# A two-layer mLSTM and GLA decoder step in one core: x stored in pieces, weight tiles requested one unit sooner, the samples' states requested over more units, GLA's last exponentials behind the gate's eviction

## The reference, cut to what matters

```python
for i in range(DEPTH):                       # DEPTH = 2, D_MODEL = 1024, D_FF = 2816
    h = rms_norm(x, g_pre_mix[i])
    mix, state = mlstm_mixer(h, ...) if i % 2 == 0 else gla_mixer(h, ...)
    x = x + rms_norm(mix, g_post_mix[i])
    h = rms_norm(x, g_pre_ffn[i])
    x = x + rms_norm(swiglu(h, w_gate[i], w_up[i], w_down[i]), g_post_ffn[i])

def swiglu(x, w_gate, w_up, w_down):
    return (silu(x @ w_gate) * (x @ w_up)) @ w_down
```

## Time and profile before

| | |
|---|---|
| median of 3 runs | 2727.17 us (2725.6 to 2729.15) |
| the profiled execution | 2726.81 us, of which 2725.0 us are the span from its first to its last instruction |
| PE busy | 2635.9 us, 97% of the span |
| ACT, DVE busy | 1009.2 us (37%), 1495.0 us (55%) |
| granted TensorE clock | mean 0.985 of full speed |
| DMA | 331.25 MB, mean 122 GB/s |

### The profile page before, as it was taken

How to read it: one execution, slowest core, us unless ns; L and a number is a source line. 1 busy time by engine, 2 the same in 40 slices (tenths; PEclk the granted TensorE clock), 3 DMA queues, 4 the chain that set the end, 5 groups by cost and what they waited for, 6 DMA issues and landing times.

```text
span 2725.0 us, 38277 instructions
## 1 busy us (share of the span) xinstructions
PE 2635.9 (97%) x15999; PEld 2383.3 (87%) x15999; DVE 1495.0 (55%) x2301; ACT 1009.2 (37%) x1439; POOL 0.2 (0%) x4
## 2 busy tenths in 40 slices
PE   7999999999999999999999999999999999999996
PEld 6899898877978998899899987998886979999996
DVE  5644475555466763356654775327676377444435
ACT  4443355432343333344423343335452334222222
POOL 0000000000000000000000000000000000000000
PEclk9999999999999999999999999999999999999998
DMA  5454454444434233443232333443335333322222
GB/s 192 137 178 143 137 170 138 132 131 143 139 112 132 85 108 103 154 131 97 90 100 93 114 117 111 139 150 115 106 103 182 112 114 127 113 84 79 86 79 84
DMA packets 181831, 331.25 MB, mean 122 GB/s; under 512 B 19580, under 2 KB 99068, under 8 KB 181660
## 3 DMA queue, kind: packets, MB, share of 16 engines
q1 hardware_dynamic: 181660, 328.81, 37.3%
HBM read 272.48 MB, written 56.28 MB: 121 GB/s over the span
## 4 chain that ended last, share of the span: by engine, by line
PE 84%; DVE 7%; ACT 4%; DMA 2%; issue 2%; SPq 0%; ACTq 0%; DVEq 0%
PE ps L837 75%; PE ps L996 2%; DMA w_stage<-w_down_in 2%; ACT w_hi L1104 1%; DVE w_lo L1411 1%; DVE Y L1504 1%; DVE n_xs L1507 1%; DVE Y L1471 1%; DVE evicted L1455 1%; PE ps L1077 1%; PE ps L949 1%; ACT hid_hi L1168 1%; PE ps L937 1%; PE ps L931 1%; PE ps L1026 1%
## 5 line engine op out<-in xcount | busy, mean ns | idle before, releaser
L837 PE MATMUL ps<-HH,w_lo 128*128 128x288 f32 (+1 forms) x3696 | 1025.2, 332 | 17.0 <-DVE HL L1905 7.4
L837 PE MATMUL ps<-HH,w_hi 128*128 128x288 f32 (+1 forms) x3696 | 1010.5, 328 | 0.0
L837 PE MATMUL ps<-HL,w_hi 128*128 128x288 f32 (+1 forms) x3696 | 1010.4, 328 | 0.0
L837 PEld LDWEIGHTS ps<-HH,w_lo 128*128 128x128 f32 x3696 | 631.7, 189 | 79.2 <-DVE w_lo L1411 17.6
L1411 DVE TENSOR_TENSOR w_lo<-w_stage,w_hi 128x1024 fp32r<-128x1024 f32 x396 | 483.6, 1221 | 367.4 <-ACT w_hi L1104 366.2
L837 PEld LDWEIGHTS ps<-HL,w_hi 128*128 128x128 f32 x3696 | 630.3, 189 | 49.3
L837 PEld LDWEIGHTS ps<-HH,w_hi 128*128 128x128 f32 x3696 | 630.4, 189 | 47.4 <-issue 0.2
L1104 ACT ACTIVATE w_hi<-w_stage 128x1024 fp32r<-128x1024 f32 x396 | 416.3, 1052 | 428.8 <-PE ps L837 292.8
L837 PE MATMUL ps<-hid_hi,w_lo 128*128 128x288 f32 (+1 forms) x1056 | 298.4, 337 | 39.4 <-issue 18.4
L1471 DVE TENSOR_TENSOR Y<-ps,Y 128x512 f32<-128x512 f32 (+1 forms) x320 | 226.9, 720 | 152.6 <-PE ps L837 152.2
L837 PE MATMUL ps<-hid_hi,w_hi 128*128 128x288 f32 (+1 forms) x1056 | 293.3, 333 | 0.0
(11 more groups left out here) (195 smaller groups left out, 1608.2 us busy)
## 6 DMA issues: line engine op xcount, KB each, us to landing
w_stage<-w_in_in SPq DMA_DIRECT2D x100, 512.0 KB, 3.8
w_stage<-w_gate_in SPq DMA_DIRECT2D x88, 512.0 KB, 3.6
w_stage<-w_up_in SPq DMA_DIRECT2D x88, 512.0 KB, 3.6
w_stage<-w_down_in SPq DMA_DIRECT2D x88, 512.0 KB, 3.9
w_stage<-w_out_in SPq DMA_DIRECT2D x32, 512.0 KB, 3.8
proj_scratch<-evicted SPq DMA_DIRECT2D x48, 288.0 KB, 2.2
proj_scratch<-evicted SPq DMA_DIRECT2D x48, 256.0 KB, 2.1
x_scratch<-n_xs SPq DMA_DIRECT2D x3, 2304.0 KB, 8.3
```

Source lines behind the costliest of these rows:

```text
L837: mm = pe.matmul(ps[:, grp.bank + t, 0:W], wsl(w, k), x[:, k, t * W:(t + 1) * W], start=(q == 0 and m == 0), stop=(q == len(ks) - 1 and m ...
```

## The change

Six edits:

1. **Weight tiles one unit sooner.** SP's unit n requests tile n + 4 instead of n + 3. It waits for the same freed slot. Tile 3 is requested ahead of three constants.
2. **x in pieces.** Each `post` of norms 2 to 7 gets a store of its own tiles (tag `xstore`), one unit behind it; the waits on `x_stored` count pieces (function `stores`). The stores of y (norms 8 and 9) stay where they were.
3. **States of the samples, layer 0.** `c_load` of the first four pieces goes out at the tags `me` of the last two prompt chunks (6 and 7), two each, instead of all four at `ma` of the sample chunk. The load of the samples' gate (`o_load`) moves to `sh(0, 0)`, the store of the prompt's state to the last `me`. In layer 1 the store of the prompt's state moves from `la` to `le`.
4. **GLA's exponentials.** Of levels 3 to 6, only level 3 stays at `la2`; 4 to 6 go to `la3`, behind the eviction of the gate unit u.
5. **GLA's arguments on DVE.** The arguments of level 3 go ahead of the two products of `la2`.
6. **The last D pair.** In the last D unit but one, PE does k = 0 of groups 0 and 1 before it waits for the second hidden tile.

```diff
+def stores(plan):
+    count, seen = 0, set()
+    for n, u in enumerate(plan.units):
+        for t in u.tags:
+            if t[0] != "post":
+                continue
+            N = plan.norms[t[1]]
...
+            count += t[3] - t[2] if N.pre is None else 1
+            N.stores = count
+            plan.tag(min(n + (N.n < 8), len(plan.units) - 1), "xstore", *t[1:])
...
-                elif k1 == KD:
-                    sp.wait_ge(s["x_added"], SUM(N.post0, KD))
-                    sp.dma_start(g.XD[:, :, toks(b)].rearrange("k p t -> p k t"), g.n.xs[:, :, 0:NT[b]]
+                else:
+                    sp.wait_ge(s["x_added"], SUM(N.post0, k1))
+                    sp.dma_start(g.XD[k0:k1, :, toks(b)].rearrange("k p t -> p k t"), g.n.xs[:, k0:k1, 0:NT[b]]
                                  ).then_inc(s["x_stored"], 16)
...
-            def ma(c):
+            def me(c):
+                if c == NC - 2:
+                    for st in range(2):
+                        c_load(0, st)
+                if c == NC - 1:
+                    for st in range(2, 4):
+                        c_load(0, st)
                 if c == NC:
                     state_out(0)
-                    o_load(NC, 0)
-                    for st in range(4):
-                        c_load(0, st)
...
+            load(3)
             sp.dma_start(g.lmask[:, :], a["c_levels"]).then_inc(s["consts"], 16)
...
-                if n + 3 < len(units):
-                    load(n + 3)
+                if n + 4 < len(units):
+                    load(n + 4)
                 evicted(u)
...
+                    if n == len(units) - 2:
+                        pe.wait_ge(s["hid_lo_ready"], hid - 1)
+                        for q in range(2):
+                            free(u.groups[q])
+                            down(q, range(1))
+                        pe.wait_ge(s["hid_lo_ready"], hid)
+                        for q in range(2):
+                            down(q, range(1, 2))
...
             def la2(c):
                 if c < NC:
-                    level_exps(c, 3, NLV)
+                    level_exps(c, 3, 4)
+
+            def la3(c):
+                if c < NC:
+                    level_exps(c, 4, NLV)
...
+                if c < NC:
+                    level_args(c, 3, 4)
                 dve.wait_ge(s["qk_landed"], 16 * (NC + 1 + c + 1))
...
                 if c < NC:
-                    level_args(c, 3, NLV)
+                    level_args(c, 4, NLV)
```

More of the change, by code:

```diff
@@ L266, in schedule @@
     tag(u, "post", 9, 0, KD)
+    stores(plan)
     order(plan)
+def stores(plan):
[5 more added lines that the diff above has]
+            N = plan.norms[t[1]]
+            if N.n not in seen:
+                seen.add(N.n)
+                N.stores0 = count
+            count += t[3] - t[2] if N.pre is None else 1
+            N.stores = count
+            plan.tag(min(n + (N.n < 8), len(plan.units) - 1), "xstore", *t[1:])
 def mlstm(plan, blk, slots):
@@ L599, in xload @@
                     sp.wait_ge(s["norm_lo"], SUM(norms[n - 1].pre0, 8))
-                    wait(sp, s["x_stored"], 16 * max(0, n - 2))
-                if n == 9:
-                    sp.wait_ge(s["x_stored"], 16 * (6 + KD))
+                wait(sp, s["x_stored"], 16 * norms[n - 1].stores)
                 wait(sp, s["y_lo"], N.mixed)
@@ L606, in xload, with xstore @@
                              ).then_inc(s["xs_landed"], 16)
-            def post(n, k0, k1):
+            def xstore(n, k0, k1):
                 N = norms[n]
@@ L676, in region_free @@
                 sp.wait_ge(s["norm_lo"], SUM(norms[n].pre0, 8))
-                wait(sp, s["x_stored"], 16 * (n - 1))
+                wait(sp, s["x_stored"], 16 * norms[n].stores)
             def mload(c):
@@ L789, in sh @@
             def sh(layer, half):
+                if layer == 0 and half == 0:
+                    o_load(NC, 0)
                 if layer == 0 and half:
@@ L818, in _ @@
             sp.wait_ge(s["y_stored"], 16 * KD)
-            sp.wait_ge(s["x_stored"], 16 * (6 + KD))
+            sp.wait_ge(s["x_stored"], 16 * norms[8].stores)
             sp.wait_ge(s["outs"], 48)
@@ L828, in _, with products @@
         def _(pe):
-            def products(hi, lo, n, wsl, ks, grp, blk, ready=None):
+            def products(hi, lo, n, wsl, ks, grp, blk, ready=None, first=0, last=None):
                 whi, wlo = g.whi[:, n % NW, :], g.wlo[:, n % NW, :]
                 W = GW[blk]
+                last = ks[-1] if last is None else last
                 for q, k in enumerate(ks):
@@ L837, in products @@
                             mm = pe.matmul(ps[:, grp.bank + t, 0:W], wsl(w, k), x[:, k, t * W:(t + 1) * W],
-                                           start=(q == 0 and m == 0), stop=(q == len(ks) - 1 and m == 2))
-                mm.then_inc(s["groups"], 1)
+                                           start=(k == first and m == 0), stop=(k == last and m == 2))
+                if ks[-1] == last:
+                    mm.then_inc(s["groups"], 1)
             def free(grp):
@@ L848, in dense, with down @@
                 if u.kind == "D":
-                    if u.j == 0:
-                        pe.wait_ge(s["hid_lo_ready"], unit("U", u.layer, b, 2 * u.i + 1).hid)
-                    for q, grp in enumerate(u.groups):
-                        free(grp)
-                        products(g.hh, g.hl, n, lambda w, k: w[:, (q * 2 + k) * P:(q * 2 + k + 1) * P], range(2), grp, b)
+                    def down(q, ks):
+                        products(g.hh, g.hl, n, lambda w, k: w[:, (q * 2 + k) * P:(q * 2 + k + 1) * P], ks, u.groups[q], b,
+                                 last=1)
+                    hid = unit("U", u.layer, b, 2 * u.i + 1).hid
+                    if n == len(units) - 2:
[6 more added lines that the diff above has]
+                            down(q, range(1, 2))
+                    elif u.j == 0:
+                        pe.wait_ge(s["hid_lo_ready"], hid)
+                    for q in range(2 if n == len(units) - 2 else 0, 4):
+                        free(u.groups[q])
+                        down(q, range(2))
                     return
```

13 lines of the change are left out of this document (8 added, 5 removed).

## The result

The changed kernel takes 2676.76 us in the median of 4 runs (2675.12 to 2677.22), the kernel before 2728.0 in runs beside it (4 runs, 2725.6 to 2729.15). The ratio is 0.9817, with a 95% interval of 0.9805 to 0.9829: 1.8% faster. The forecast was 2680, in a range of 2667 to 2696. The profiled execution took 2676.7 with a span of 2674.9, so the span is 50.1 us shorter than before. PE is busy for 2620.0 us, 98% of the span, at a mean clock of 0.993.

A forecast was written before the change was run, and what follows sets the result against it. PE, busy for 97% of the span, was taken to bound the kernel, so only its idle time and lost clock could be won. Gains of 29.4 + 8.2 + 5.0 + 1.2 + 3.3 = 47.1 us gave 2680, range 2667 to 2696.

The forecast's parts named there:

- Stores of x: Four places where x is stored: late down tiles stall PE; gaps and lost clock go, 29.4 us, lower bound 14.9.
- Pieces still collide: Rival: two of the four store stalls stay, half of 29.4, giving 2694 us; chance 0.14.
- Start: Seventh unit: PE's gap of 7.07 us shrinks to 1.6 and the clock holds, 8.2 us gained.
- Samples: Layer 0's first sample step: down tile in time, PE's gap of 5.84 falls to 2.4; 5.0 us gained with clock.
- GLA beside 576 columns: One gap of 2.9 becomes two of about 2: 0 for the gap, 2.4 us lost to the clock.
- GLA beside 512 columns: Chunks 5 to 7: PE no longer waits for the gate's eviction, 1.2 us gained per chunk, 3.6 in all.
- Last D pair: PE fills the gap of 2.40 with 12 matmuls, leaving 0.1 and 0.7: 3.3 us gained with clock.
- Costed at nothing: Same bytes, 21 more issues in SP's idle time, later tags with units in hand: no cost.
- rival of the fixed price: Each piece's transfer has 2.6 us fixed; if tiles cannot move then, 21 more cost 55 us: 2735; chance 0.04.
- SP's waits on x: Rival: 27 waits on x_added in SP's queue, formerly six, hold back tiles; with half the pieces 2800 us; chance 0.04.
- GLA's gaps go too: Rival: ACT's queue has unseen slack, 10 us more gained, giving 2669 us; chance 0.10.
- Table loads: ACT's chain: trace shows 1.28 us per load without drain; by the skill's page the GLA sum would be 5.5 smaller.

The follow-up runs named there:

- early_only: The kernel before with only the weight tiles requested one unit sooner, x still stored whole: 2685.32 us, ratio 0.985.
- unsplit: The changed kernel with only the pieces undone, x stored whole at the old place: 2679.43 us, ratio 0.9827.
- split_only: The kernel before with only x stored in pieces one unit later, weight tiles requested at the old place: 2695.23 us, ratio 0.9883.
- prep: The changed kernel with DVE's preparation of layer 0's first sample step one unit earlier: 2672.5 us, ratio 0.9803.
- start: The changed kernel with the seventh weight tile and the second block's x requested ahead of the second projected tile's store: 2673.37 us, ratio 0.9806.
- pair_old: The changed kernel with PE again waiting for both hidden tiles in the last D unit but one: 2679.03 us, ratio 0.9828.
- exps_l1: The changed kernel with ACT's exponentials of levels 4 to 6 later still, behind hi of the second down unit: 2670.08 us, ratio 0.9795.
- args_l1: The kernel of exps_l1 with DVE's arguments of levels 4 to 6 also moved behind the first D unit's evictions: 2666.87 us, ratio 0.9781.
- args_old: The changed kernel with level 3's arguments back behind the two products on DVE, the late exponentials kept: 2690.56 us, ratio 0.9869.

## Why the prediction was right

The forecast's sum was 47.1, the traces show 50.1. Term by term:

- **Stores of x**, 29.4 forecast, 30.1 measured. The mechanism, a request behind a wait, is shown by early_only, unsplit and split_only in so far as a sooner request removed the stall each time; that the store's bytes had their part in the length of the stall, as the prediction also said ("Store and tiles share the DMA engines"), is seen in unsplit. What the prediction did not see is that edits 1 and 2 each do it alone (split_only has all 30.1, early_only 27.8); the rival "Pieces still collide" feared something that the sooner requests had made harmless. The bank that DVE frees late costs 0.72, not 0.3.
- **Start**, 8.2 forecast, 5.8 measured. The gap was put at 1.6 and is 2.64 in this execution, and the clock fell. The same queue gave 1.54 to 2.03 in eight other executions (those with edit 1 and the start unchanged), at six of which the clock held. In those eight the whole term was 7.3 to 9.4 us, so 8.2 was right for most and 5.8 is the low one. The size hangs on when the tile lands beside 2304 KB of x: 9.5 to 10.0 us from request to `hi` in the eight, 10.6 in this one. The step that failed here is "at which the clock holds".
- **Samples**, 5.0 forecast, 6.7 measured. The gap is 2.27 where 2.4 was said; I left 1.7 for the clock, and it held. In eight other executions with this gap it held once and fell seven times, so my allowance was right for most and too high for this one.
- **GLA beside 576 columns**, 0 for the gap and 2.4 for the clock forecast, 0.3 lost in all. Two gaps in place of one, for DVE's Y, as foretold. The clock fell behind them in two of three chunks. I had counted that as an extra cost of 2.4 and left out that behind the three single gaps of before it had fallen each time too (0.84, 0.83 and 0.83 over 10 us), which the change could give back. That the result is near nothing is in part luck: in four other traces with this order, unsplit and prep lose 0.3 and 0.1 beside 576 columns, start and pair_old 2.7 and 2.4, which is what was forecast.
- **GLA beside 512 columns**, 3.6 forecast, 3.9 measured, with the waits of 0.7 for `k_decayed` at their place.
- **Last D pair**, 3.3 forecast, 2.9 measured, and 0.9 more since the last norm's matmuls ran at full clock (1.24 us for 2.17). pair_old shows 1.9 of gap; the rest is clock, and not the same in each execution: behind the gap of 2.40 it held in three of the four traces that have it.
- **Costed at nothing.** The 21 more transfers cost nothing that shows: with the store whole the time is 2679.43, not under 2676.76. The Trainium skill, "DMA: Bandwidth & Descriptors", "Rules for kernel authors", wants at least 1 MiB in a transfer for the most bandwidth. The trace agrees for the single transfer, since 288 KB of x take 2.1 us from issue to landing where 2304 KB took 8.3; for the kernel's time it does not matter here, where stores of 256 to 864 KB lie beside PE's work. The rival of the fixed price falls. (The 2.0 us that the prediction took for it from the Trainium skill's fit, same page, "Anatomy of one DMA", are given there for DMAs issued from GpSimd, and these are SP's.) So does that of SP's waits on x: no tile behind a piece made PE wait. Edit 3's states were costed at nothing for PE, and the prediction put the gain down to "the tile in time"; early_only bears that out. The rival "GLA's gaps go too" was put aside because ACT's chain has no idle row; exps_l1 and args_l1 show that the gaps go or shrink (1.42 to nothing, 1.94 to 0.80) once work is moved out of the chains of ACT and DVE.
- **Table loads.** ACT's exponentials start 0.02 us behind a load of 1.28 in args_old (1221.18 and 1222.48). The Trainium skill, "ScalarE: Activation LUTs", "What ACT_TABLE_LOAD costs", adds 1.38 of drain; this case's traces show none, here as in the earlier trace rows, and none ahead of the load either (it starts at 1221.18, where the eviction of 1220.52 has ended after 0.65).

The case was right in its mechanisms. Its sum was only 3 us short because errors between -2.4 and +2.1 us in its terms partly cancelled, and three of these (start -2.4, samples +1.7, GLA +2.1) hang on when a tile landed and how the clock fell in the one execution that was traced. What it got wrong in kind is that GLA's two edits were taken as one sum: by the medians their halves are a loss of 9 us and a gain of 14. Two slips in its working change nothing: the upper bound of GLA's sum is 18.8, not 18, and what the range leaves over is 0.12, not 0.13.

## What to carry to other kernels

A wait in an in-order DMA queue delays every request behind it; look at what stands behind it, when that is due, and how long it lands beside the bytes that the wait lets go. A request that goes out sooner by more than the sharing costs needs nothing else. When a chain is cut, price each half alone: a table load more on the path is a loss until the wait in front of it is shortened too. After a change, read the new releaser of each gap that is left: here three of them (ACT's order, SP's queue at the start, DVE's preparation) gave another 17.6 us, for moves of a line or two.

## What the runs showed of the hardware

The granted clock behind a gap of about 2 us does not follow from the gap's length. The place ahead of W's first unit had a gap of 2.22 in all fourteen profiled executions: behind it the clock of 10 us was 0.83 to 0.86 in ten and 1.00 in four. The gap of 2.25 to 2.27 ahead of the samples was followed by 0.66 in four executions, 0.83 in three and 1.00 in two; that of 2.40 ahead of the last pair by 0.83 in one and 1.00 in three. All twelve of 1.67 to 1.69 beside 512 columns were followed by 1.00, and of GLA's gaps of 2.85 to 2.92 beside 576 eleven of twelve by 0.83 to 0.86. Shorter gaps are not safe either: the waits of 0.78 and 0.80 for `l_k` in args_old were followed by 0.83 in two of three chunks. So a gap near 2 us costs itself and, at times, 1.7 to 3.4 us more, and a single trace tells only one draw of it. These are executions of fourteen kernels that are alike at these places; what decides is not shown.
